# Another order of the pieces in three attention stages of a two-block transformer kernel, and squares for the norms summed over three pairs on VectorE

## The reference, cut to what matters

```python
# first block, each of 2 layers; xc is the context, left out after the last layer's projections
h  = modulate(rms_norm(x, norm1_g[l]), sh1, sc1)
hc = modulate(rms_norm(xc, norm1_g[l]), csh1, csc1)
q, k, v, up, ca, cb = project_inputs(h, w_in[l], q_norm_g[l], k_norm_g[l])
...
attn = diff_attn_post(diff_attention(q, k_all, v_all, lam), subln_g[l], lambda_init)
pool_o = pool_mixer(up, pool_w[l], pool_scale[l])
conv_o = conformer_conv(ca, cb, conv_dw_w[l], conv_dw_b[l], conv_ln_g[l], conv_ln_b[l])   # 31 taps, layer norm, silu
x = x + g1 * jnp.einsum('blm,md->bld', concat([attn, pool_o, conv_o]), w_out[l])
x = x + g2 * swiglu(modulate(rms_norm(x, norm2_g[l]), sh2, sc2), w_ffn_in[l], w_ffn_out[l])
# the same for xc, in layer 1 only
...
# second block, each of 2 layers
h = rmsnorm(x, attn_norm[l])
c_q, c_kv, k_r, q_d, k_d, v_d = jnp.split(h @ w_in[l], split_at, axis=-1)
mixed = concat([mla_mixer(...), dilated_attention(...)])
x = x + mixed @ w_out[l]
x = x + conv_ffn(rmsnorm(x, ffn_norm[l]), ...)
```

## Time and profile before

| what | value |
|---|---|
| median of 3 runs | 1672.39 us (1670.56 to 1675.26) |
| the profiled execution's own time | 1672.15 us |
| its span, first to last instruction | 1670.3 us |
| mean granted TensorE clock | 0.990 |
| PE busy | 1607.1 us, 96% |
| DVE busy | 1112.2 us, 67% |
| ACT busy | 922.6 us, 55% |
| POOL busy | 156.7 us, 9% |

### The profile page before, as it was taken

How to read it: one execution, slowest core, us unless ns; L and a number is a source line. 1 busy time by engine, 2 the same in 40 slices (tenths; PEclk the granted TensorE clock), 3 DMA queues, 4 the chain that set the end, 5 groups by cost and what they waited for, 6 DMA issues and landing times. The chain is left out here.

```text
span 1670.3 us, 31133 instructions
## 1 busy us (share of the span) xinstructions
PE 1607.1 (96%) x12918; PEld 1476.0 (88%) x12918; DVE 1112.2 (67%) x1736; ACT 922.6 (55%) x1467; POOL 156.7 (9%) x136
## 2 busy tenths in 40 slices
PE   5999999999999999998899999998999999999999
PEld 3987479999999999965799999878999998789999
DVE  2799667645566655887664456777887567778873
ACT  3444756545464444546454446766665467666662
POOL 1230000111001110300011100000011000001010
PEclk8999999999999999998999999999999999999999
DMA  9443765666546554464366554213555642235553
GB/s 382 166 152 127 262 243 204 254 228 218 192 176 214 188 191 172 152 243 163 107 197 203 191 187 166 94 55 125 202 190 189 225 142 91 77 128 204 195 192 123
DMA packets 45164, 301.09 MB, mean 180 GB/s; under 512 B 5232, under 2 KB 7504, under 8 KB 11744
## 3 DMA queue, kind: packets, MB, share of 16 engines
q1 hardware_dynamic: 44304, 297.44, 50.2%
q0 software_dynamic: 288, 0.92, 0.1%
q10 hardware_dynamic: 432, 0.75, 0.1%
HBM read 298.02 MB, written 1.06 MB: 179 GB/s over the span
## 5 line engine op out<-in xcount | busy, mean ns | idle before, releaser
L2009 DVE TENSOR_TENSOR wl<-raw,wh 128x1040 fp32r<-128x1040 f32 (+1 forms) x472 | 569.8, 1245 | 319.0 <-ACT wh L1762 225.0
L1762 ACT ACTIVATE wh<-raw 128x1040 fp32r<-128x1040 f32 (+1 forms) x472 | 465.4, 1031 | 180.5 <-PE bank L1551 94.7
L1546 PE MATMUL bank<-hx_hi,wh 128*128 128x256 f32 x1856 | 523.2, 282 | 7.3 <-ACT hx_hi L1762 7.3
L1551 PE MATMUL bank<-hx_lo,wh 128*128 128x256 f32 x1856 | 516.4, 278 | 0.0
L1549 PE MATMUL bank<-hx_hi,wl 128*128 128x256 f32 x1856 | 515.3, 278 | 0.1
L1546 PEld LDWEIGHTS bank<-hx_hi,wh 128*128 128x128 f32 x1856 | 349.8, 188 | 13.7 <-issue 12.8
L1549 PEld LDWEIGHTS bank<-hx_hi,wl 128*128 128x128 f32 x1856 | 349.8, 188 | 4.3 <-issue 3.8
L1551 PEld LDWEIGHTS bank<-hx_lo,wh 128*128 128x128 f32 x1856 | 349.7, 188 | 0.7 <-DVE hx_lo L2002 0.4
L1546 PE MATMUL bank<-hid_hi,wh 128*128 128x256 f32 x912 | 252.7, 277 | 1.4 <-ACT hid_hi L1762 1.3
L1549 PE MATMUL bank<-hid_hi,wl 128*128 128x256 f32 x912 | 252.2, 277 | 0.9 <-DVE wl L2009 0.9
L1551 PE MATMUL bank<-hid_lo,wh 128*128 128x256 f32 x912 | 252.2, 276 | 0.2
(11 more groups left out here) (220 smaller groups left out, 1936.8 us busy)
## 6 DMA issues: line engine op xcount, KB each, us to landing
raw<-in_wts SPq DMA_DIRECT2D x208, 1032.0 KB, 4.9
raw<-in_wts SPq DMA_DIRECT2D x50, 1024.0 KB, 6.7
raw<-in_wts SPq DMA_DIRECT2D x20, 776.0 KB, 4.2
raw<-in_wts SPq DMA_DIRECT2D x4, 584.0 KB, 4.6
tmp<-tscr SPq DMA_DIRECT2D x16, 128.0 KB, 3.9
raw<-in_wts SPq DMA_DIRECT2D x2, 648.0 KB, 3.9
xTc<-in_ctxT SPq DMA_DIRECT2D x1, 1024.0 KB, 10.8
xTx<-in_xT SPq DMA_DIRECT2D x1, 1024.0 KB, 7.2
```

The lines of the kernel that those rows point to most:

```text
L1546: pe.matmul(out, block(f, M.wh, w0 + k, ncols, c, m), x_hi, start=first and k == 0 and o == 0, stop=False, skip_group_check=True)
L1551: ins = pe.matmul(out, block(f, M.wh, w0 + k, ncols, c, m), x_lo, start=False, stop=last and k == nk - 1, skip_group_check=True)
L1762: return act.activation(out, in_, func, bias=bias, scale=scale)
L2009: tt(M.wl[k][:, cols], M.raw[r][:, cols], M.wh[k][:, cols].bitcast(F32), ALU.subtract).then_inc(*on.inc(lo))
```

## The change

Three things. The table for layer 2 of the first block is another. The table for the second block's layers is another. And the squares are summed on DVE: instead of POOL's three adds over two pairs, DVE adds whole 128x512 tiles of up to three pairs and at last folds the result's halves (`add_last`, `nadd`). An add is issued one call of `add()` later than its square, or by `root()`. Seven of the ten norms of this kind sum three pairs, so that PE's root has 3 matmuls in place of 5; the three behind the first block's out projections sum two pairs (`Norm(s, 2)`) and keep 5.

```diff
-IN_SECOND = ("K m P m", "P m K m", "P m S x m", "N A m Z m", "O m", "O m", "", "", "", "", "", "")
-BETWEEN = ("r D0 L0 L2 N r s r D2 D4 r D3", "", "D1 r r Q0 K0", "", "h", "s V Q1", "r r", "K1 r D5 s", "",
...
+IN_SECOND = ("K P s s", "m P", "K S m", "x", "N h m h A m", "Z P s s", "m h m", "", "t O m", "", "m O", "")
+BETWEEN = ("h r D0 h L0 L2 N r r D2 D4 r D3", "", "D1 r r Q0", "K0", "", "s K1 h s V Q1", "r r", "s r D5 h h", "h r",
...
-        def __init__(self, s, pooled=True):
+        def __init__(self, s, pooled=3):
...
-            sums = [ev("nacc") for _ in range((1, 2, 0, 0)[self.n - 1] if self.pooled else 0)]
...
+            step("nsq", s=self.s, pair=pair, q=q, free=q.free, ready=ready, t=t)
+            self.add_last()
+            if self.n <= self.pooled:
+                self.open = self.n, q, t
+            else:
                 self.late.append((q, t))
+
+        def add_last(self):
...
+            if self.open:
+                n, q, t = self.open
+                if n == 1:
+                    self.acc, self.t_acc = q, t
+                else:
+                    sums = [ev("nacc") for _ in range(2 if n == self.pooled else 1)]
+                    step("nadd", fold=n == self.pooled, q=q, acc=self.acc, t=t, ready=self.t_acc, sums=sums)
+                    self.t_acc = sums[-1:]
+                    tmps.give(q, sums[0])
+                self.open = None
...
         def root(self):
+            self.add_last()
...
-                        norm[s] = Norm(s)
+                        norm[s] = Norm(s, 2)
...
-    n = {s: Norm(s, pooled=s == "c") for s in "cx"}
+    n = {s: Norm(s, pooled=3 * (s == "c")) for s in "cx"}
...
+    def nadd(fold, q, acc, t, ready, sums):
+        A, B = acc.t[:, 0:T], acc.t[:, T:2 * T]
+        on.wait_ge(ready, t[0])
+        tt(acc.t[:, :], acc.t[:, :], q.t[:, :], ALU.add).then_inc(*on.inc(sums[0]))
+        if fold:
+            on.wait_ge(sums[0])
+            tt(A, A, B, ALU.add).then_inc(*on.inc(sums[1]))
...
-    def nsq(n, q, acc, t, sums, before, **_):
-        if not sums:
-            return
-        A = acc.t[:, 0:T]
-        if n == 1:
-            on.wait_ge(t)
-            tt(A, A, q.t[:, T:2 * T], ALU.add).then_inc(*on.inc(sums[0]))
-        elif n == 2:
-            on.wait_ge(t, before)
-            tt(A, A, q.t[:, 0:T], ALU.add).then_inc(*on.inc(sums[0]))
-            on.wait_ge(sums[0])
-            tt(A, A, q.t[:, T:2 * T], ALU.add).then_inc(*on.inc(sums[1]))
```

More of the change, by code:

```diff
@@ L275 @@
             "s m t T h m Z Y t O h h", "h O s m m", "O m", "O m", "", "m", "m")
-IN_SECOND = ("K m P m", "P m K m", "P m S x m", "N A m Z m", "O m", "O m", "", "", "", "", "", "")
-BETWEEN = ("r D0 L0 L2 N r s r D2 D4 r D3", "", "D1 r r Q0 K0", "", "h", "s V Q1", "r r", "K1 r D5 s", "",
-           "r Q2 Q3 s h", "h", "h r K2 r r K3", "s h r", "O0 s O1", "", "O2", "", "h s O3", "",
-           "h h T0 T1 s T2 T3 h")
+IN_SECOND = ("K P s s", "m P", "K S m", "x", "N h m h A m", "Z P s s", "m h m", "", "t O m", "", "m O", "")
+BETWEEN = ("h r D0 h L0 L2 N r r D2 D4 r D3", "", "D1 r r Q0", "K0", "", "s K1 h s V Q1", "r r", "s r D5 h h", "h r",
+           "Q3 Q2 h", "", "s K2 r r r K3 h", "s", "r O0 h O1 s", "", "O2", "", "h O3 h", "h", "h s T0 T1 T2 T3 h")
 BY_HALF, BY_COLS = [(1, 0), (1, 1), (0, 0), (0, 1)], [(0, 0), (1, 0), (0, 1), (1, 1)]
@@ L459, in plan_program @@
     class Norm:
-        def __init__(self, s, pooled=True):
+        def __init__(self, s, pooled=3):
             self.s, self.n, self.rs, self.late, self.pooled, self.acc, self.t_acc = s, 0, None, [], pooled, None, None
-            self.raw, self.wait, self.keep = [], None, False
+            self.raw, self.wait, self.keep, self.open = [], None, False, None
         def add(self, pair, ready, single=False):
@@ L470, in add @@
             self.n += 1
-            sums = [ev("nacc") for _ in range((1, 2, 0, 0)[self.n - 1] if self.pooled else 0)]
[L472 to L480, removed]
-                self.late.append((q, t))
+            step("nsq", s=self.s, pair=pair, q=q, free=q.free, ready=ready, t=t)
[3 more added lines that the diff above has]
+            else:
+                self.late.append((q, t))
+        def add_last(self):
[9 more added lines that the diff above has]
+                self.open = None
         def unscaled(self, pair, ready, gain, out, out_free):
@@ L1581, in nroot @@
         if acc:
-            mm(b.t[:, 0:T], M.ones, acc.t[:, 0:T], True, False)
+            ins = mm(b.t[:, 0:T], M.ones, acc.t[:, 0:T], True, not late)
         for n, (q, t_q) in enumerate(late):
@@ L2268, in gate2 @@
         tt(yu.t[:, :], yg.t[:, :], yu.t[:, :], ALU.mult).then_inc(*on.inc(m))
-    walk(plan, {"init": init, "split": split, "nraw": nraw, "scaled": scaled, "nfin": nfin, "modend": modend, "hn2": hn2, "qn2": qn2, "glu": glu, "tap": tap,
+    walk(plan, {"init": init, "split": split, "nadd": nadd, "nraw": nraw, "scaled": scaled, "nfin": nfin, "modend": modend, "hn2": hn2, "qn2": qn2, "glu": glu, "tap": tap,
                 "conv1": conv1, "conv2": conv2, "exp1": exp1, "wt1": wt1, "sub1": sub1, "pcsplit": pcsplit,
@@ L2334, in store @@
             pool.dma_start(io["out"][:, c:e, :], M.xT["x"][:, c:e, :]).then_inc(*on.inc(t, 16))
-    walk(plan, {"init": init, "nsq": nsq, "pool": pools, "hidsplit": hidsplit, "gate2": gate2, "lora1": lora1,
+    walk(plan, {"init": init, "pool": pools, "hidsplit": hidsplit, "gate2": gate2, "lora1": lora1,
                 "store": store})
```

## The result

| | before | changed |
|---|---|---|
| median | 1671.47 us (4 runs) | 1656.26 us (4 runs, 1654.61 to 1657.02) |
| profiled execution, own time | 1672.15 us | 1654.61 us |
| its span | 1670.3 us | 1652.8 us |
| mean granted clock in it | 0.990 | 0.994 |

The ratio is 0.9902, with a 95% interval from 0.989 to 0.9914: about 1% faster, 15.2 us between the medians. The forecast was 1661.5, 10.7 less than before.

What follows compares the result with a forecast made beforehand. PE, busy 96%, was taken as the bound, so only its work, waits or low clock could be won. -8.8 - 1.7 + 1.1 - 1.3 = -10.7 from 1672.15 gave 1661.5; band 1656 to 1666 (0.60), range taking in 1652 to 1670.

Steps and rivals of the forecast that it cites:

- Stretch of layer 2: First scores to last out-projection pieces in the first block's layer 2: new table ends it at 790.6, not 799.5, -8.8.
- R1: Rival: DVE and ACT bound layer 2's stretch, so waits only move; 1667, from 1665 to 1670; chance 0.20 with R4.
- the list of remaining waits: Layer 2's stretch: PE still waits 3.1 behind the scores, 3.1 at the mean matmul, 2.3 and 0.8, together 9.3.
- The work of the stretch: Layer 2's stretch: 83.1 less 12.9 of waiting and 5.3 of clock is 64.9, or 67.0 with two modulation pieces.
- Cover by the v GEMM: Layer 2: the v GEMM of x, 5.9 on PE, moved beside ACT's convolution chain, removes the 4.42 wait for hc_hi.
- Norms at the ends of the first block's FFNs: End of the first FFN for c and for x in layer 1: two matmuls fewer each, 2 x 0.85, -1.7.
- Four unscaled transitions: Where the next GEMM's first half runs on unscaled x: fewer matmuls only lengthen PE's wait for hx_hi, 0.
- End of layer 2's out projection: Add and fold on DVE between third and fourth residual pair, covered by nothing: 0.69 + 0.42, +1.1.
- Table of block two: Split before the last out-projection pieces taken earlier, so the 0.64 wait goes in both layers: -1.3; the rest 0.
- R3: Rival: merged waits in layer 2's stretch drop the clock over the v GEMM and two out pieces, 1681.8; chance 0.08.
- R2: Rival: v GEMM and out pieces cover all waits of layer 2's stretch, 1652; chance 0.12.
- R4: Rival: the change of norms is all there is and the tables do nothing, 1671.5; counted into R1's upper end.

Runs made afterwards that it cites:

- v_moved: Kernel before, with the v GEMM of x alone moved from row 2 to row 3 of layer 2's table, ahead of the first out-projection piece: 1672.37 us, ratio 1.0.
- o_moved: Kernel before, with the two first out-projection pieces alone moved from rows 4 and 5 to rows 8 and 10 of layer 2's table: 1671.15 us, ratio 0.9988.
- v_early: Changed kernel, with the v GEMM of x alone put back to row 2 of layer 2's table: 1661.21 us, ratio 0.9929.
- norms_only: Changed kernel with both old tables, so only the sums of squares moved from POOL to DVE: 1671.62 us, ratio 0.9987.
- second_only: Kernel before with the new table of layer 2 alone: 1660.84 us, ratio 0.9921.
- tables_only: Kernel before with both new tables, sums of squares still on POOL: 1657.92 us, ratio 0.9905.
- between_only: Kernel before with the new table of block two alone: 1668.02 us, ratio 0.9963.
- pooled2: Changed kernel, with two pairs summed on DVE at every norm that had three by default (the context's first norm keeps three): 1659.54 us in one run.
- s_moved: Kernel before, with one weight split in block two's table moved from between T1 and T2 to ahead of T0: 1670.87 us in one run.

## Why the prediction was right, point by point

The result lies in the range, 0.3 above the lower end of the band of 1656 to 1666 that was given 0.60, and on the side forecast. By its steps:

- **Stretch of layer 2: -8.8 forecast, -11.6 found.** The wait for hc_hi and the loss of clock behind it went, as predicted, and R1 is refuted for the whole table, though not for its parts (v_moved, o_moved). The mis-sized step is the list of remaining waits: 9.3 forecast, 6.7 found. The wait behind the first scores was to be 3.1 and is 0.69 + 0.60, since the piece's split on ACT no longer stands between the exps and the norm. Mean matmul and transposes: 3.1 forecast, 1.31 + 1.89 found. The first head's norm: 2.3 forecast, 1.26 found. The rest, 0.8, came as 0.47 twice. That the remaining waits would cost no clock was wrong: behind 1.31 and 1.89 the changed kernel fell to the lower level, and over the whole stretch its clock of 0.98 is, as an estimate, 1.5 us of 73.6. The work of the stretch was put about as much too high, since before its clock of 0.92 over 83.1 is 6.6 us and not 5.3. The two errors cancel, which is luck.

```profile
744.40:748.40 4.00, 4.00 (x22) 1.69 (x20) 2.41 (x7) 3.32 (x9) 0.00 (x0) 0.62 0.00 0
```

- **Cover by the v GEMM.** Not borne out by itself. In the old table the move gave nothing (v_moved). In the new one 6.2 us of the stretch hang on its place (v_early), but by the split on ACT at the norm of k1 (3.7) and by the clock (2.5): the waits where it was to be the cover are the same in sum with it and without it. The prediction left out that a GEMM that moves takes its split along. Neither v_moved nor o_moved reaches the gain of the table; which other letters are needed beside them was not tested.
- **Norms at the ends of the first block's FFNs: -1.7 forecast**, -1.83 in norms_only. In the changed kernel it is hidden: the scores come at 714.38, not 712.5. Two things take it back. A wait of 0.7 for ACT's tmp at 707.83, of which before has none, comes with the new table (second_only and tables_only have it too; second_only starts its scores 0.9 later than its moved pieces account for). And a drift of 1.0 by the root at 261 us (261.64 for 260.65) is 1.4 in between_only and v_moved, which have no edit there, so it is none of the change.
- **Four unscaled transitions: 0 forecast.** Right as to the matmuls: pooled2 shows that two more or fewer only change PE's wait. Wrong as to the sums: the prediction said of POOL's adds that nobody waits for them. PE doesn't; DVE is held up by them, 0.57 per layer at block two's out projections, once the split that hid it is gone (norms_only: nothing with the old table; changed against tables_only: 31.19 for 31.77).
- **End of layer 2's out projection: +1.1 forecast, +0.4 in the changed kernel, +0.5 in norms_only.** The 1.1 of DVE is there, but the sum left out what POOL's adds had cost at this very place: 0.5, by which they stretched the split (2.88 before, 2.38 in norms_only). It is the same step as in the point above.
- **Table of block two: -1.3 forecast, -4.6 in between_only.** This is the largest error of the sum. The step said that one wait of 0.64 goes. In fact the path there is the chain of 11.2 behind the third residual, and the waits of 0.64 and 2.28 in the earlier trace rows were both its shadow: with the third residual 2.3 earlier the first is gone, the second is 1.29, and the end comes 2.3 earlier. s_moved confirms that the place of the split ahead of that residual is worth 1.2 of it. The prediction took PE's listed wait as the price, not what DVE did ahead of the residual.
- **Clock.** R3 did not happen: the v GEMM ran at full clock, since the drop behind 1.31 and 1.89 was over by 748. Not in the sum was that the low clock behind hx_hi of layer 2's FFN would be absent in the changed kernel, up to 1.7 by the clock of 0.68 there (below); with other small shifts it is taken to account for the 0.9 between the -3.8 of that row of the table and the 2.85 measured at its end (from the transposes to hx_hi, 34.04 and 31.19).
- **Rivals.** R2 (all waits go, 1652) was missed by the 6.7 us that stay. R4, that the tables do nothing, is refuted by tables_only.

The 17.5 are from one execution of each kernel, the medians say 15.2. The 6.8 between -10.7 and -17.5 are 2.8 in the stretch, 4.4 in block two (its table and the POOL adds), 0.7 at the out projection and 0.9 of clock, less 1.8 for the norms' gain that was hidden and 0.2 at the end. So the time came within the range although three terms were off by 2.8, 4.4 and 1.8.

## What to carry to other kernels

Where a GEMM is moved to cover a chain, move its weight split in the same thought: here the split runs on the engines of the chain that was to be covered, and the wait only turned up somewhere else. When PE waits at the end of a stage, follow the chain back on the slower engines to the last point where it had slack, and price the edit there, not by PE's wait. An engine that nobody waits for can still slow a neighbour: look at the same instruction's length with and without it running.

## What the runs showed of the hardware

Two DVE instructions hid_lo (two inputs in SBUF each) take 0.89 alone and 1.46 with POOL's adds of 128x256 beside them; in s_moved, with two POOL adds falling on them, 1.69. The two half splits wl<-raw,wh take 2.38 alone and 2.88 with one such add. The second hid_lo of tables_only starts 0.12 behind a POOL add and takes twice its 0.48:

```profile
1139.20 0.95 DVE L2001 SCALAR_TENSOR_TENSOR hid_lo<-xTx,vec,hid_hi 128x256 fp32r<-128x256 f32 x1
```

The Trainium skill (SBUF — State Buffer, Who interferes with whom) has it that a DVE instruction with two SBUF inputs contends with a GpSimd instruction that reads SBUF, and that the later one waits. These rows agree that the DVE instruction that starts later is the one that loses; what it loses, 0.47 here and 0.51 at the split, is less than what was left of POOL's add by its record, 0.68 and 0.65.

The same wait does not always have the same effect on the clock. At the norm of k1 behind the first scores PE waits 2.50 in v_moved and goes on at full clock, and waits 2.49 in norms_only and goes on at the lower level for its four matmuls (busy time by stretch, v_moved, then norms_only):

```profile
726.00:731.00 5.00, 2.50 (x15) 0.97 (x14) 3.75 (x5) 4.33 (x8) 0.00 (x0) 1.00 0.53 175
```
```profile
726.00:731.00 5.00, 4.42 (x12) 2.36 (x13) 5.00 (x11) 3.50 (x7) 0.00 (x0) 0.66 0.88 319
```

The matmuls bank<-tmp,cst there take 1.98 at full clock and 3.66 in norms_only. In the first matmuls on hx_hi of layer 2's FFN it is the other way round: behind 2.17 the kernel before fell in the next microseconds (first row below, clock 0.68), and behind 2.12 the changed kernel did not (the other two, 1.00):

```profile
817.20:822.20 5.00, 4.98 (x28) 4.82 (x29) 5.00 (x13) 3.05 (x7) 0.00 (x0) 0.68 0.07 17
804.00:809.00 5.00, 2.88 (x21) 2.65 (x21) 3.83 (x10) 3.28 (x7) 0.00 (x0) 1.00 0.00 0
809.00:814.00 5.00, 5.00 (x42) 4.93 (x41) 4.27 (x9) 4.14 (x7) 0.00 (x0) 1.00 0.13 36
```

In these kernels such a drop cost 1.4 to 2.2 us, so profiles of the same stretch in two kernels are to be compared with their clocks beside them. What decides between a drop and none was not tested and stays open.
